# A two-layer scan backbone: 32-row exponent products in the state-space scan, and modulation rows turned on VectorE

## The reference

```python
sh1, sc1, g1, sh2, sc2, g2 = jnp.split(silu(c) @ mod_w[i] + mod_b[i], 6)
...
ac = jnp.cumsum(da.reshape(b, nc, CHUNK, g, e), axis=2)
seg = ac[:, :, :, None] - ac[:, :, None]
decay = jnp.exp(jnp.where(tril[:, :, None, None], seg, -jnp.inf))
scores = jnp.einsum('bclgn,bcsgn->bclsg', cc, bc)[..., None] * decay
y_diag = jnp.einsum('bclsge,bcsgep->bclgep', scores, xc)
...
s_start = ...   # state carried from chunk to chunk
y_off = jnp.einsum('bclgn,bcgepn->bclgep', cc, s_start) * jnp.exp(ac)[..., None]
```

## Time and profile before

| | us |
|---|---|
| median of 3 runs | 1884.34 |
| lowest, highest | 1884.04, 1887.13 |
| the profiled execution | 1884.42 |
| its span, first to last instruction | 1882.6 |
| PE busy in the span | 1802.7 (96%) |
| DVE busy | 1151.3 (61%) |
| ACT busy | 640.3 (34%) |
| POOL busy | 127.2 (7%) |
| mean granted TensorE clock | 0.99 |

### The profile page before, as it was taken

The page is one execution under the profiler, slowest core; times in us unless marked ns, Lnnn a source line. Parts: engine busy times, 40 slices in busy tenths (PEclk is TensorE's granted clock), DMA queues, the critical chain, the costliest instruction groups (busy, mean ns, idle before and its releaser), DMA issues. The chain is left out here.

```text
span 1882.6 us, 35011 instructions
## 1 busy us (share of the span) xinstructions
PE 1802.7 (96%) x14348; PEld 1436.7 (76%) x14348; DVE 1151.3 (61%) x2295; ACT 640.3 (34%) x1474; POOL 127.2 (7%) x122
## 2 busy tenths in 40 slices
PE   6999999998998999999999999999989998999997
PEld 2447777887667868888888878887766666989997
DVE  2653676534787553445544377776859868766765
ACT  4121223633552031111100043675256876132210
POOL 0000232000000100000001000001211111000000
PEclk9999999999999999999999999999989999999999
DMA  7433201123402322222233132222222011534443
GB/s 304 179 117 137 90 23 45 56 102 143 151 4 90 146 68 90 89 78 82 88 140 134 67 109 87 74 68 91 91 92 91 2 40 65 203 132 170 157 168 101
DMA packets 28174, 195.99 MB, mean 104 GB/s; under 512 B 3020, under 2 KB 4301, under 8 KB 5870
## 3 DMA queue, kind: packets, MB, share of 16 engines
q1 hardware_dynamic: 27970, 193.61, 28.8%
q10 hardware_dynamic: 44, 0.14, 0.0%
HBM read 192.69 MB, written 1.05 MB: 103 GB/s over the span
## 5 line engine op out<-in xcount | busy, mean ns | idle before, releaser
L2015 ACT ACTIVATE ws_sb<-psum 128x256 f32<-128x256 f32 (+4 forms) x446 | 187.1, 421 | 851.6 <-PE psum L946 820.5
L946 PE MATMUL psum<-arena_sb,ws_sb 128*128 128x256 f32 (+3 forms) x2208 | 377.9, 323 | 2.4 <-DVE hT_sb L2664 0.9
L946 PEld LDWEIGHTS psum<-arena_sb,ws_sb 128*128 128x128 f32 (+1 forms) x2208 | 317.0, 183 | 42.3 <-issue 13.8
L946 PE MATMUL psum<-hT_sb,ring_sb 128*128 128x256 f32 (+3 forms) x1344 | 326.9, 390 | 2.4 <-ACT hT_sb L2015 1.8
L946 PEld LDWEIGHTS psum<-hT_sb,ring_sb 128*128 128x128 f32 (+1 forms) x1344 | 228.3, 189 | 80.9 <-issue 57.4
L2664 DVE TENSOR_TENSOR ws_sb<-ws_sb,psum 128x256 f32<-128x256 f32 (+2 forms) x310 | 121.2, 400 | 186.7 <-PE psum L946 86.1
L946 PE MATMUL psum<-arena_sb,ring_sb 128*128 128x256 f32 (+1 forms) x1168 | 214.2, 333 | 3.1 <-ACT arena_sb L2015 1.7
L946 PEld LDWEIGHTS psum<-arena_sb,ring_sb 128*128 128x128 f32 x1168 | 183.7, 191 | 22.4 <-DVE ws_sb L2664 2.7
L2664 DVE TENSOR_TENSOR ws_sb<-ring_sb 128x512 f32<-128x512 f32 (+1 forms) x166 | 116.4, 701 | 103.3 <-PE psum L946 72.6
L946 PE MATMUL psum<-ring_sb,hT_sb 128*128 128x256 f32 (+4 forms) x1024 | 168.4, 347 | 0.8 <-ACT hT_sb L2015 0.8
L946 PEld LDWEIGHTS psum<-ring_sb,hT_sb 128*128 128x128 f32 (+1 forms) x1024 | 135.9, 174 | 37.6 <-issue 17.2
(11 more groups left out here) (226 smaller groups left out, 2262.9 us busy)
## 6 DMA issues: line engine op xcount, KB each, us to landing
ring_sb<-w SPq DMA_DIRECT2D x142, 1024.0 KB, 4.9
arena_sb<-w SPq DMA_DIRECT2D x12, 1024.0 KB, 15.1
hT_sb<-w SPq DMA_DIRECT2D x12, 1024.0 KB, 4.9
ring_sb<-w SPq DMA_DIRECT2D x8, 768.0 KB, 4.4
xT_sb<-x SPq DMA_DIRECT2D x2, 2048.0 KB, 10.0
const_sb<-w SPq DMA_DIRECT2D x3, 1024.0 KB, 6.7
const_sb<-consts SPq DMA_DIRECT2D x1, 2048.0 KB, 10.1
extra_sb<-w SPq DMA_DIRECT2D x1, 1024.0 KB, 7.0
```

Source lines behind the costliest of these rows:

```text
L946: return nc.tensor.matmul(o, l, r, start=start, stop=stop, **kw)
L2015: return nc.scalar.activation(o, i, func, **kw)
```

## The change

Exponents. The running sums of da are made once for all steps (`running_sums`, 8 small products inside unit 2 of `qk0`), from da and its negative (`da_signed`); ACT spreads them into `moving_sums` and `fixed_sums` on rows 64 to 127 of `wide`. POOL now makes one operand of 64x512 a step (`head_sums`). An exponent is then a difference of running sums: a product over 32 rows, one for each direction, on rows 64 to 95 and 96 to 127, into banks 4 and 5 at once. The two directions are no longer added but the smaller one is taken: ACT copies bank 5 into `e_seg` (`backward_copied`), DVE takes the minimum with bank 4 (`least`), ACT exponentiates in place. Both gate halves are now scaled by ACT (eight copies), and DVE adds them in one operation. The exponent products of step w + 1 stand behind the z0 products of step w, and wait for `least(w)`.

Modulation. For the twelve pieces DVE transposes the bank in 32x32 blocks straight out of PSUM, in place of ACT's copy; PE makes one product of 32 columns with a selecting matrix (`added_parts`), which adds the four partial sums; DVE adds the bias in four operations on 32 rows each (`with_bias`). At the pauses both transposes come behind the 8 or 16 scaled tiles of `norm` on DVE.

The diff, cut to its core:

```diff
@@ PE: modulation
-                for t in range(4):
-                    last = nc.tensor.transpose(psum[:, 5, t * P:(t + 1) * P], late_row[:, t * P:(t + 1) * P], ident)
-                last.then_inc(S["late_columns"], 1)
+                added_parts(5, late_row).then_inc(S["late_columns"], 1)
...
+            def added_parts(bank, turned_rows):
+                return mm(psum[:, bank, 0:32].rearrange("p (b r) -> p b r", r=2), cm("pick"),
+                          turned_rows.rearrange("p (b r) -> p b r", r=32)[:, :, 0:2])
...
+            def running_sums():
+                pe.wait_ge(S["ssd_signed"], 1)
+                for j in range(TT):
+                    for d in DIRS:
+                        last = mm(psum[64 + 32 * d:96 + 32 * d, 6, j * P:(j + 1) * P], da_signed[:, j, d].rearrange("p a b -> p (a b)"), upto_incl[d])
+                last.then_inc(S["dt_turned"], 1)
@@ PE: the loop
                 def decay(w):
-                    if w > 1:
-                        pe.wait_ge(S["ssd_exp"], w - 1)
+                    if w > 0:
+                        pe.wait_ge(S["ssd_least"], w)
+                    pe.wait_ge(S["ssd_r"], w + 1)
+                    j = w // 4
                     for d in DIRS:
-                        u = 2 * w + d
-                        pe.wait_ge(S["ssd_r"], u + 1)
-                        mm(psum[:, 4 + w % 2, :], beyond[d], g_decay[:, d].rearrange("p a b -> p (a b)"),
-                           start=(d == 0), stop=(d == 1)).then_inc(S["ssd_seg"], 1)
+                        rows_ = slice(64 + 32 * d, 96 + 32 * d)
+                        last = mm(psum[:, 4 + d, :], wide[rows_, 2, j * P:(j + 1) * P], head_sums[rows_, w % 2].rearrange("p a b -> p (a b)"))
+                    last.then_inc(S["ssd_seg"], 1)
...
@@ ACT: the loop
+                def backward_copied(w):
+                    act.wait_ge(S["ssd_seg"], w + 1)
+                    if w > 1:
+                        act.wait_ge(S["ssd_p"], w - 1)
+                    own(f(e_seg[:, w % 2].rearrange("p a b -> p (a b)"), psum[:, 5, :], ACT.Copy).then_inc(S["ssd_copied"], 1), S["ssd_copied"])
+                backward_copied(0)
                 for w in range(16):
...
                     for i in range(4):
                         h = h0 + i
-                        ins = f(g_dt[:, w % 2, i], g_mask[:, 1, g, j], ACT.Copy, scale=dt[:, j, 16 + h:17 + h])
+                        f(g_dt[:, w % 2, i], g_mask[:, 1, g, j], ACT.Copy, scale=dt[:, j, 16 + h:17 + h])
+                        ins = f(g_dt_fwd[:, w % 2, i], g_mask[:, 0, g, j], ACT.Copy, scale=dt[:, j, h:h + 1])
                     own(ins.then_inc(S["ssd_dt"], 1), S["ssd_dt"])
-                    act.wait_ge(S["ssd_seg"], 2 * w + 2)
-                    own(f(e_seg[:, w % 2], psum[:, 4 + w % 2, :].rearrange("p (a b) -> p a b", a=4), ACT.Exp).then_inc(S["ssd_exp"], 1), S["ssd_exp"])
+                    act.wait_ge(S["ssd_least"], w + 1)
+                    own(f(e_seg[:, w % 2], e_seg[:, w % 2], ACT.Exp).then_inc(S["ssd_exp"], 1), S["ssd_exp"])
+                    if w + 1 < 16:
+                        backward_copied(w + 1)
...
@@ DVE
+            def pause_turned(tag):
+                layer, first, banks = PAUSES[tag]
+                for k in range(2):
+                    arrived, turned = (S["mod_rows"], S["mod_copied"]) if layer else (S["late_rows"], S["late_turned"])
+                    dve.wait_ge(arrived, first + k + 1 - (0 if layer else MOD_FIRST))
+                    own(V.transpose(wide[:, k, :], psum[:, banks[k], :]).then_inc(turned, 1), turned)
+            def with_bias(layer, at, bank):
+                parts = psum[:, bank, 0:32].rearrange("p (t u r) -> p t u r", u=4, r=2)
+                bias = cl("mod_b", 48 * layer + at, 4)
+                for u in range(4):
+                    rows_ = slice(32 * u, 32 * u + 32)
+                    ins = tt(mod[rows_, layer, at:at + 4], parts[rows_, :, u], bc(bias[rows_], 2, 2), ALU.add)
+                return ins
...
+                def least(w):
+                    dve.wait_ge(S["ssd_copied"], w + 1)
+                    e = e_seg[:, w % 2].rearrange("p a b -> p (a b)")
+                    own(tt(e, e, psum[:, 4, :], ALU.min).then_inc(S["ssd_least"], 1), S["ssd_least"])
+                least(0)
                 inputs(0)
                 for w in range(16):
                     scores(w)
+                    if w + 1 < 16:
+                        least(w + 1)
                     if w > 0:
                         accumulate(w - 1)
...
+            da_by_way = da.rearrange("p j (d h) -> p j d h", d=2)
+            link(copy(da_signed[:, :, :, 0], da_by_way))
+            own(ts(da_signed[:, :, :, 1], da_by_way, -1.0, None, ALU.mult).then_inc(S["ssd_signed"], 1), S["ssd_signed"])
```

More of the change, by code:

```diff
@@ L453, in backbone @@
         g_dt = area(ws, 5120, 2, 4, P)
+        g_dt_fwd = area(extra, 0, 2, 4, P)
+        sum_rows = slice(64, P)
+        moving_sums, fixed_sums = wide[sum_rows, 1, :], wide[sum_rows, 2, :]
+        plus_col, minus_col = (cl("sum_ways", n)[sum_rows] for n in range(2))
         xw = [area(w, at, SSD_H, SSD_P) for w, at in ((ws, 6144), (extra, 1024))]
@@ L987, in between @@
                     turn_dt()
+                if stage == "qk0" and g == 2:
+                    running_sums()
                 for half in LATE_AT.get((stage, g), ()):
@@ L1144, in mod1_columns @@
                     pe.wait_ge(S["mod_taken"], q)
-                row = wide[:, q - 4, :] if q in (4, 5) else mod_piece
+                if q in (4, 5):
+                    added_parts(7, wide[:, q - 4, :]).then_inc(S["mod_columns"], 1)
+                    return
                 for t in range(4):
-                    last = nc.tensor.transpose(psum[:, 7, t * P:(t + 1) * P], row[:, t * P:(t + 1) * P], ident)
+                    last = nc.tensor.transpose(psum[:, 7, t * P:(t + 1) * P], mod_piece[:, t * P:(t + 1) * P], ident)
                 last.then_inc(S["mod_columns"], 1)
@@ L1168, in pause_columns @@
                 layer, first, banks = PAUSES[tag]
-                copied, columns = (S["mod_copied"], S["mod_columns"]) if layer else (S["late_copied"], S["late_columns"])
+                turned, columns = (S["mod_copied"], S["mod_columns"]) if layer else (S["late_turned"], S["late_columns"])
                 for k in range(2):
[L1171 to L1174, removed]
+                    pe.wait_ge(turned, first + k + 1 - (0 if layer else MOD_FIRST))
+                    added_parts(banks[k], wide[:, k, :]).then_inc(columns, 1)
+            def added_parts(bank, turned_rows):
+                return mm(psum[:, bank, 0:32].rearrange("p (b r) -> p b r", r=2), cm("pick"),
+                          turned_rows.rearrange("p (b r) -> p b r", r=32)[:, :, 0:2])
             def keep_clock(n):
@@ L2793, in besides @@
                         link(ts(neg_eg, eg, -1.0, None, ALU.mult))
+                    if stage == "xbc" and t in (2, 6, 10):
+                        late_turned(t // 4)
                     if stage == "xbc" and t in (6, 9):
```

85 lines of the change are left out of this document (41 added, 44 removed).

## The result

The changed kernel takes 1946.7 us (median of four runs, 1943.9 to 1948.1), the kernel before in the same comparison 1885.7: ratio **1.0315, 95% interval 1.0293 to 1.0338**. The prediction was 1924, with a range up to 1943. The direction and most of the mechanism were right; the time lies 23 us above the forecast and just outside the range. The profiled execution has a span of 1945.5 us, 62.9 more than before.

The account below looks back on a forecast made before the run. It took TensorE (PE), busy 96% of the span, as the bound. Loop plus 29.1, clock plus 11.2 and the rest minus 1.0 make 39.3 us on 1884.42: 1924 us, range 1908 to 1943.

Parts of the forecast that it names:

- What bounds the kernel, the waits: State-space loop: PE, the bound, waits for `accumulate`: 3.77 us in full steps (four operations), 2.31 short (two), 1.59 copy (one).
- The pair of shallow products: Exponent products in the loop: two 32-row products overlap, 0.86 us instead of 1.72, plus 0.15 per step for entering the mode.
- The loop at full clock: State-space loop without clock loss: steps longer by 31.9 us in sum, start 2.8 earlier, so plus 29.1 us.
- The clock: Loop waits lower PE's clock: 1.2 us lost in each of eight full steps, 0.8 in two short ones, plus 11.2.
- The rest: Outside the loop: modulation products minus 2.6, sign copies 0.5, bias adds 0.2, running sums 0.9; sum minus 1.0 us.
- The bias adds: Query stage: four DVE operations instead of one, at the one place where PE waits for them, plus 0.2 us.
- the sign copies: Query stage: two 128x128 sign copies on DVE, with the transpose behind `dt`, may bring some 0.5 us to PE.
- The clock that holds: Rival, in the loop: the new waits leave the clock alone, 29.1 - 1.0, 1912 us; chance 0.08.
- the pairs that don't overlap: Rival, in the loop: shallow exponent products run one after the other, 15 x 0.86 us more, 1937 us; chance 0.08.
- The clock stays low: Rival, in the loop: waits every 11 us come before the clock settles, 4.6 us each, 1951 us; chance 0.08.
- The other side: Rival, in the loop: `accumulate` not held up, PE-bound, each step saves 0.86 - 0.15 us, 1873 us; chance 0.04.

Follow-up runs that it names:

- order-only kernel: The changed kernel with one move on DVE, `least(w+1)` behind `accumulate(w-1)` instead of ahead of it: 1879.4 us, ratio 0.9953 to the kernel before.
- the filled kernel: The changed kernel plus 1 to 3 unread products of constants on PE in the waits of steps 1 to 14: 1918.9 us, ratio 1.0161.
- the kernel with pairs: The changed kernel plus unread products of constants in PE's loop waits, except in steps 3, 4, 11 and 12: 1929.2 us, ratio 1.0234.
- the one with four waits: The changed kernel plus unread products of constants in PE's loop waits, except in steps 4, 6, 12 and 14: 1932.0 us, ratio 1.0241.
- modulation alone: The kernel before with only the modulation part of the change, its loop as before: 1886.3 us, ratio 1.0001 (0.9991 to 1.0012).

## Why the prediction was wrong
**What bounds the kernel, the waits.** Right. PE was the bound, and the waits came at the predicted places, released by the predicted instruction. Each is 0.36 shorter than predicted (3.40, not 3.77): the diagonal products last 1.10 us until PE is idle, where 0.84 was taken, and the chain is 0.1 shorter.

**The pair of shallow products.** Right that they overlap: the next product starts 1.06 us after the pair does, predicted 0.86 + 0.15. The neighbours' 0.10 each weren't predicted. With the 0.20 of the pair itself (1.06 less 0.86) that makes 0.40 a step instead of 0.15, which no wait hides in the order-only kernel. The Trainium skill ("TensorEngine Tiling (Array Packing)", Key Properties) says that changing the mode drains TensorE. The 0.40 are in line with that, but no run separates how much of them is such a drain.

**The loop at full clock.** Right. Predicted plus 29.1; the filled kernel, which has the same chain and the clock at 1.00, shows plus 30.7. It isn't luck: a full step is 3.15 us longer than before (245.73 to 256.67 between diagonal products, against 7.78), where 3.06 was predicted.

**The clock.** This is the step that failed: the term for the low clock was mis-sized, 11.2 us in place of 24.8. The prediction took "3.4 us at 1.2 instead of 2.4 GHz" from the one fall in the earlier trace rows, and went on: "In the row the fall came about when the wait ended; in a longer wait a part of the low time is waited off", so 1.2 us for a full wait, 11.2 in all. The first half is what the runs show as well: some of the low time does pass while PE waits. But where the fall comes deep inside the wait (0.7 us or more ahead of its end) the stretch is 6.8 us and not 3.4, and the wait costs more clock, not less. In the kernel after, seven of the eight full waits had 6.8 us, the eighth full wait, two short ones and one copy step had 3.4 each: 61.4 us low. Of this 11.1 lie inside the waits (1.4 to 1.9 each), and (61.4 - 11.1) / 2 = 25.2 us are lost, where the filled kernel says 24.8. The same sum gives 10.9 for the kernel with pairs (measured 11.0, loop against the filled one's) and 10.6 for the one with four waits (10.7). A full wait costs 2.6 us of clock in seven of eight cases, not 1.2. With 24.8 for the clock, and all else as it stood, the forecast would have been 1938.

Also, 1.59 us was to be short enough to keep the clock in the copy steps, since a wait just under 2 us had kept it. With 1.23 us it was lost in one of four. One row of each kind was taken for a rule, and the range built on it was too narrow. The trace of the kernel before had other rows. Around a wait of 1.89 us, shorter than the one that had kept the clock, it shows a low stretch of 6.8 us (timeline and windows, kernel before):
```profile
1589.32 1.97 PE L1400 MATMUL psum<-const_sb,hT_sb 128*128 128x128 f32 x8 [1.89 <-DVE hT_sb L2667]
```
```profile
1588.00:1590.00 2.00, 0.68 (x3) 0.68 (x4) 1.86 (x5) 1.81 (x10) 0.73 (x1) 0.74 0.00 0
1590.00:1592.00 2.00, 1.53 (x8) 1.10 (x7) 1.80 (x6) 1.87 (x6) 0.00 (x0) 0.50 0.00 0
1592.00:1594.00 2.00, 1.92 (x9) 1.55 (x9) 1.81 (x6) 1.23 (x3) 0.00 (x0) 0.50 0.00 0
1594.00:1596.00 2.00, 2.00 (x11) 1.92 (x11) 1.90 (x4) 1.18 (x2) 0.00 (x0) 0.55 0.33 45
```
So both the longer stretch and the fall at a short wait could have been seen beforehand.

**The rest.** Predicted minus 1.0. In the profiled execution the time outside the loop grew by 7.3 us, the second part of the miss. By the sum above all of it would be clock: low for 50.6 us there, 2.7 of them inside waits, and for 37.5 with 5.5 before, so 24.0 us are lost against 16.0, 8.0 more. How much of that belongs to the change isn't shown. It scatters from one execution to the next (19.4 and 23.7 us in the two of the order-only kernel), and the ratio of the runs, 59 us, leaves some 4 beside the loop's 55.6, with an interval of 0 to 8. Ahead of the loop 1.1 arose, less than the place of the loop's start moves between executions (204.8 to 208.5). The bias adds (predicted plus 0.2) made their wait 0.4 longer, and a low stretch of 3.4 came with it, 1.7 us lost; added up, that is most of the 2.6 that the shorter products were to give. By these terms (minus 2.6, plus 0.2) modulation alone had a ratio of 0.9987, just outside the interval measured. The 0.5 for the sign copies was right (the wait near 170 us went from 0.68 to 1.21).

**The rivals.** The clock that holds (1912) and the pairs that don't overlap (1937) didn't come. "The clock stays low" (1951) is the nearest in time and half right: the clock came back to 1.00 in each step, but cost 2.6 per full wait instead of 1.2. The other side (`accumulate` not held up) is what the order-only kernel makes true: 1879.4, above the 1873 of the prediction, since the loop gains 7.7 us and not 10.7: a step takes 6.46 us instead of 6.92 (260.82 to 267.28 between diagonal products), 0.46 less and not 0.71.

## What to carry to other kernels
When an instruction that waits for another engine is put ahead of one that the bound engine needs, add up the whole chain behind it and look for its cover: here it cost 3.4 us in a full step, and moving it one place down, or its producer one block up, gave a kernel slightly faster than the one before (by 0.3 to 0.5% and by 0.1%). New waits on TensorE cost clock as well as their own length; take that price from several such waits and keep its spread in the range, since waits of 1.2 to 3.5 us cost anything from nothing to 3 us of clock here. Where such a wait can't be taken away, even products that nobody reads are worth having in it (28 us here).

## What the runs showed of the hardware
- In or behind waits of 1.2 to 2.5 us the granted clock fell in some cases and held in others: 3 of 6 at 1.23 to 1.32, 4 of 9 at 1.57 to 1.68, 3 of 8 at 2.48; at 3.4 to 3.5 it fell in all 20.
- In and right behind the loop a low stretch lasted 3.4 us where the clock fell about when the wait ended or later, and 6.8 where it fell 0.7 us or more ahead of that. Elsewhere in the program this doesn't hold: 10.2 us in four kernels whose clock fell 1.2 to 1.5 us behind a wait of 1.55, and 13.7 us around the wait of 5.3 to 5.6 us in all kernels but one, which had 17.1. The Trainium skill ("TensorE: Matmul & The Clock Gate", HAM oscillation) describes a kernel whose waits take the clock down each time anew; the full waits of the kernel after agree, and the shorter ones here do so only in part.
- A pair of products over 32 rows, on two row groups and into two banks, 512 columns each, takes 1.06 us until the next product starts, against 1.72 for two over 128 rows one behind the other; the full-height products ahead of and behind it take 0.10 longer each.
